# Attention of two heads at a time, and the state input of the S5 mixer on ScalarE's queue

## The chip, the cores and the metric

The kernel runs on one core of one Trainium2 chip. The time is the device time of one execution in microseconds (us). The engines are TensorE (PE; its weight loads are PEld), VectorE (DVE), ScalarE (ACT), GpSimd (POOL) and SyncE (SP), whose queue issues most of the DMAs.

## What is computed

Two blocks of a network over 512 tokens of 1024 features, in float32. The first pools, then runs a gated feed-forward layer with a short convolution. The second has two layers. Layer 0 mixes tokens by forgetting attention, layer 1 by an S5 state space model, and each ends in a gated feed-forward layer. What the change touches is the attention and the entry of S5:

```
def fox_mixer(h, w_in, b_f, q_gain, k_gain, w_out):      # 16 heads of 64
    proj = h @ w_in                                      # q, k, v, gate, f_logit
    q = rmsnorm(heads(q), q_gain); k = rmsnorm(heads(k), k_gain); v = heads(v)
    c = jnp.cumsum(log_sigmoid(f_logit + b_f), axis=1)
    for blk in range(seq_len // Q_BLOCK):                # 4 blocks of 128 queries
        s = einsum('bhqd,bhkd->bhqk', qb, kb) * scale + c[q] - c[k]
        s = where(mask, s, -inf)                         # causal
        p = softmax(s, axis=-1)
        outs.append(einsum('bhqk,bhkd->bhqd', p, vb))
    return (concatenate(outs) * sigmoid(gate)) @ w_out

def s5_mixer(h, w_in, ...):
    u = h @ w_in       # states from u, then outputs from the states and from u
    ...
    y = gelu(y + d_skip * u)
    return (y * sigmoid(y @ w_glu)) @ w_out
```

## The kernel before

Every large product is split in three passes: a weight tile is divided into a high and a low part (`w_hi` by ACT in `hi`, `w_lo` by DVE in `lo`), the activations into `hh` and `hl`, and PE runs high by high, high by low and low by high (`passes`, L1742 to L1744). A slot is one weight tile of 128x1024: 8 steps of 128 by three passes are 24 matmuls of 512 columns. Five slots lie in a ring (`RING`). SP loads slot n when slot n-5 is done, and `hi` and `lo` of slot n+3 are written beside slot n (`LEAD`).

Each engine runs its own program in the order in which it is written, with semaphores between them. In `fox` the loop over i takes the heads by pairs. A pair's q and k lie in `qk`, head 0 on partitions 0 to 63, head 1 on 64 to 127. For each i PE runs three slots of the next pair (n, n+1, n+2: q, k, gate), and between them the steps of the pair i, one head at a time:

- `scores(jj, head)`: for each of four query blocks `qb`, of 512, 128, 384 and 256 columns, three matmuls of q with k over 64 rows (L1989 to L1991), the causal mask over 128 rows (L1992), and the forget table `c_tab` over 48 rows (L1993). All five have one head's half of the rows, but the mask.
- DVE `row_max` (L1325), ACT `attend_exp` (L916), DVE `normalize` (L1335).
- `transposes` (L2005): ten blocks of 128x128 of `prob`, then ACT and DVE split them into `pt_hi` and `pt_lo`.
- `values`: 12 matmuls into bank 7, then DVE `head_out` multiplies with the gate and splits the result.
- `head_sums` (L2034): the sums of squares of q and k of the next pair, two float32 matmuls that give four records, after the scores of head 1. ACT then takes a logarithm and an exponential for the norm, DVE makes `qk` (`make_qk`).

`scores` of a pair waits for both halves of its `qk` (`qk_done`). After the last pair `fox_out` runs the output product.

POOL makes rotation tables for S5 beside this loop. SP stores one every second slot.

In `s5` the input product u comes out in 8 slots of 512 columns. `evict_u` (ACT) copies each to `us`. SP writes it to DRAM (`u_write`, L655) and reads it back in another order (`u_read`, L661) into `ub`. PE needs `ub` in `states(i)` (L2137) and `inside(i)` (L2147). DVE runs the recurrence between, and `across_two` (L2152) adds the states' outputs, with the two halves of the rows in turn. SP's queue also carries w1, turn, w3 (8 DMAs each, L645) and q2 tables, the weights, and the even trips of y (`y_write`, `y_read` with 8 DMAs; the odd ones are on ACT's queue). At the start of S5 SP first waits for all table stores and issues four w3 tables before the weight slots 1 to 4 of S5.

## Time and profile before

| | |
|---|---|
| runs shown | 1893.88, 1901.82, 1902.87 us (median 1901.82) |
| profiled execution | 1896.73 us, its span 1895.0 us |
| mean granted clock of TensorE in it | 0.937 |
| PE busy | 94% of the span |
| DVE, ACT, POOL busy | 55%, 34%, 12% |

Times in the profile count from the first instruction. The span is cut into stretches below, and for each the busy time of each engine and the granted clock of TensorE are read. The clock has two levels, 2.4 GHz (granted 1.00) and 1.2 GHz (0.50). A value between is a mean over the stretch. "xN" behind an engine's time counts its instructions, those that reach into the stretch included.

### The profile page before, as it was taken

What the parts mean: (1) busy time and instruction counts of PE and PEld (TensorE: products, weight loads), DVE (VectorE), ACT (ScalarE), POOL (GpSimd) and SP (SyncE); (2) the same over time, 40 slices, a digit from 0 to 9 for tenths busy, and PEclk for the clock granted to TensorE, in tenths of its full rate; (3) what the DMA queues carried; (4) which work ended last, traced back from release to release, by engine and by line L of the source; (5) the groups of instructions that cost most, each with busy time, mean ns of one, the idle gap of its engine ahead of it and who ended that gap; (6) DMA issues with size and microseconds to landing.
All of it is one profiled execution on the core that took longest, in us unless ns stands there. A gap on an engine that the chain in (4) does not pass through costs nothing.

```text
span 1895.0 us, 22168 instructions
## 1 busy us (share of the span) xinstructions
PE 1772.6 (94%) x8681; PEld 1466.2 (77%) x8681; DVE 1040.9 (55%) x1575; ACT 637.5 (34%) x1000; POOL 228.5 (12%) x757
## 2 busy tenths in 40 slices
PE   2749999999999999999999999997979999999998
PEld 2738888888787777777888888886868888888886
DVE  5988766676645555555734335665652653433323
ACT  3335433323434434343522222233213442222222
POOL 5001520000037423431000000000011000000000
PEclk7569999999999888888999999998969999999999
DMA  9443323334442111211322323445864233223332
GB/s 382 153 170 100 100 91 99 100 123 139 117 123 65 47 43 39 62 37 48 114 91 99 100 93 119 123 131 179 236 180 141 67 123 100 100 91 98 100 92 75
DMA packets 138151, 212.69 MB, mean 112 GB/s; under 512 B 29904, under 2 KB 104000, under 8 KB 134848
## 3 DMA queue, kind: packets, MB, share of 16 engines
q1 hardware_dynamic: 132864, 209.18, 34.9%
q10 hardware_dynamic: 5184, 2.10, 0.4%
q8 instruction: 69, 1.13, 0.2%
q14 instruction: 34, 0.28, 0.0%
HBM read 193.43 MB, written 17.82 MB: 111 GB/s over the span
## 4 chain that ended last, share of the span: by engine, by line
PE 81%; DVE 7%; DMA 4%; SPq 3%; ACT 2%; POOL 1%; issue 1%; ACTq 0%; DVEq 0%; PEldq 0%; POOLq 0%
PE bank L1742 24%; PE bank L1743 24%; PE bank L1744 24%; DMA u_scratch<-us 2%; SPq L645 2%; DVE ada L1161 1%; PE bank L1993 1%; DMA rcnt<-in_rcnt 1%; ACT prob L916 1%; DVE w_lo L1075 1%; PE bank L1989 1%; PE bank L1873 1%; PE bank L1782 1%; PE bank L2147 1%; DVE rinv L1325 1%
## 5 line engine op out<-in xcount | busy, mean ns | idle before, releaser
L1742 PE MATMUL bank<-hh,w_hi 128*128 128x512 f32 (+1 forms) x1440 | 560.9, 390 | 17.7 <-DVE w_lo L1075 14.0
L1743 PE MATMUL bank<-hl,w_hi 128*128 128x512 f32 (+1 forms) x1440 | 551.6, 383 | 0.0
L1744 PE MATMUL bank<-hh,w_lo 128*128 128x512 f32 (+1 forms) x1440 | 551.0, 383 | 0.0
L1075 DVE TENSOR_TENSOR w_lo<-raw,w_hi 128x1024 fp32r<-128x1024 f32 x264 | 318.4, 1223 | 241.7 <-ACT w_hi L732 238.3
L732 ACT ACTIVATE w_hi<-raw 128x1024 fp32r<-128x1024 f32 x264 | 278.7, 1057 | 394.9 <-PE bank L1744 123.9
L1742 PEld LDWEIGHTS bank<-hh,w_hi 128*128 128x128 f32 x1440 | 275.5, 191 | 74.3 <-DVE w_lo L1075 15.2
L1743 PEld LDWEIGHTS bank<-hl,w_hi 128*128 128x128 f32 x1440 | 275.0, 191 | 53.4 <-issue 3.0
L1744 PEld LDWEIGHTS bank<-hh,w_lo 128*128 128x128 f32 x1440 | 274.2, 190 | 52.8
L1742 PE MATMUL bank<-w_hi,hid 128*128 128x512 f32 x528 | 207.1, 392 | 0.0
L1744 PE MATMUL bank<-w_hi,hid 128*128 128x512 f32 x528 | 205.6, 389 | 0.0
L1743 PE MATMUL bank<-w_lo,hid 128*128 128x512 f32 x528 | 205.4, 389 | 0.0
L1221 DVE TENSOR_TENSOR scr<-scr,bank 128x512 f32<-128x512 f32 x44 | 30.3, 688 | 289.8 <-PE bank L1744 289.8
L1742 PEld LDWEIGHTS bank<-w_hi,hid 128*128 128x128 f32 x528 | 99.1, 188 | 22.1 <-issue 1.7
L824 ACT ACTIVATE scr<-bank 128x512 f32<-128x512 f32 x44 | 26.3, 598 | 266.8 <-PE bank L1744 266.8
L1744 PEld LDWEIGHTS bank<-w_hi,hid 128*128 128x128 f32 x528 | 99.1, 188 | 20.9
L1743 PEld LDWEIGHTS bank<-w_lo,hid 128*128 128x128 f32 x528 | 99.2, 188 | 20.2
L811 ACT ACTIVATE scr<-bank,convw 128x512 f32<-128x512 f32 x44 | 34.4, 781 | 139.3 <-PE bank L1744 139.3
L1737 POOL TENSOR_TENSOR hl<-yfm,hh 128x512 fp32r<-128x512 f32 x8 | 10.9, 1388 | 571.5 <-ACT hh L1004 571.5
L1197 DVE SCALAR_TENSOR_TENSOR scr<-bank,convw,scr 128x511 f32<-128x511 f32 x44 | 33.0, 749 | 64.6 <-ACT scr L811 64.6
L916 ACT ACTIVATE prob<-bank,nmax 128x128 f32<-128x128 f32 (+1 forms) x64 | 32.9, 526 | 105.2 <-DVE nmax L1327 105.2
L1161 DVE CUSTOM_DVE_ANT_0 ada<-ada,csil 128x1024 f32<-128x1024 f32 x48 | 57.6, 1255 | 12.6 <-DMA ada<-in_ada_w 12.4
L1594 POOL TENSOR_TENSOR turn_new<-turn_t 128x2 f32<-128x2 f32 (+2 forms) x192 | 55.4, 288 | 15.0
(271 smaller groups left out, 2204.0 us busy)
## 6 DMA issues: line engine op xcount, KB each, us to landing
raw<-in_up SPq DMA_DIRECT2D x132, 512.0 KB, 3.3
raw<-in_dn SPq DMA_DIRECT2D x60, 512.0 KB, 4.1
ada<-in_ada_w SPq DMA_DIRECT2D x24, 1024.0 KB, 9.6
raw<-in_fox_in SPq DMA_DIRECT2D x32, 512.0 KB, 3.9
raw<-in_s_w SPq DMA_DIRECT2D x24, 512.0 KB, 4.5
q_scratch<-q_tab SPq DMA_DIRECT2D x8, 512.0 KB, 4.3
w_scratch<-w_new SPq DMA_DIRECT2D x8, 512.0 KB, 5.1
raw<-in_fox_out SPq DMA_DIRECT2D x8, 512.0 KB, 3.7
```

Source lines behind the costliest of these rows:

```text
L645: sp.dma_start(w3[s::BLK, i % TABS, :, :], k_dram[i][:, :, at_s:at_s + P]).then_inc(w3_in[i % TABS], 16)
L732: act.activation(w_hi[:, n % RING, :], raw[:, n % RING, :], ACT.Copy).then_inc(hi_done, 1)
L811: act.activation(scr[:, 2 * s, :], bank[base + (2 * j + s) % 4][:, :], ACT.Identity, scale=convw[:, j, 4 * s + 1:4 * s + 2], bias=convw[:, ...
L916: act.activation(prob[:, P_AT[qb]:P_AT[qb] + w], S_AT[qb], ACT.Exp, bias=nmax[:, qb:qb + 1], accum_out=rsum[:, qb:qb + 1]).then_inc(exp_do ...
L1075: dve.tensor_tensor(w_lo[:, n % RING, :], raw[:, n % RING, :], w_hi[:, n % RING, :].bitcast(F32), ALU.subtract).then_inc(lo_done, 1)
L1161: dot = dve.tensor_tensor_reduce(wt, wt, csil[:, :], 1.0, 0.0, ALU.mult, ALU.add, accum_out=dots[:, 2 * b + t:2 * b + t + 1])
L1197: own.add(dve.scalar_tensor_tensor(c[:, 1:T], b[:, 0:T - 1], convw[:, j, 4 * s:4 * s + 1], c[:, 1:T], ALU.mult, ALU.add))
L1221: dve.tensor_tensor(p, scr[:, j % 2, :], bank[base + (2 * j + 1) % 4][:, :], ALU.mult)\
L1594: own.add(pool.tensor_tensor(out_, a, b, op))
L1742: pe.matmul(dst, w_h, r_h, start=first, stop=False, skip_group_check=True)
L1743: pe.matmul(dst, w_h, r_l, start=False, stop=False, skip_group_check=True)
L1744: return pe.matmul(dst, w_l, r_h, start=False, stop=last, skip_group_check=True)
```

## The change

The two heads of a pair now go through every step together.

- Scores: `two_scores` issues each matmul of head 0 and head 1 in turn, on rows 0 to 63 and 64 to 127, into different banks. The table comes before the mask. Block sizes are paired as (512, 512), (384, 256), (128, 384), (256, 128).
- Softmax in two groups: `WIDE` holds the two blocks of 512, `REST` the other six. Maxima, exponentials and reciprocals are made by group.
- All 20 transposes stand behind slot n+1, all 24 value matmuls behind slot n+2.
- The sum of squares of q stands in the middle of slot n+1, that of k behind the transposes. ACT and DVE make q before k is there.
- `head_out` handles both heads in one copy and one subtraction.
- In S5, ACT issues the write and the read of u. SP issues two w3 and two q2 tables before the weight slots 1 to 4, and waits for the table stores only behind a third w3 table.

```diff
-        S_AT = [bank[2][:, 0:P], bank[3][:, 0:2 * P], bank[2][:, P:4 * P], bank[4][:, :]]
+        def s_at(h, qb):
+            return (bank[4 + h][:, 0:P], bank[6][:, 2 * P * h:2 * P * h + 2 * P], bank[4 + h][:, P:4 * P],
+                    bank[2 + h][:, :])[qb]
...
+        WIDE, REST = [(0, 3), (1, 3)], [(0, 2), (1, 2), (0, 1), (1, 1), (0, 0), (1, 0)]
+        HS_BANK = [bank[7], bank[1]]
...
-            def u_write(i):
-                sp.wait_ge(ut_done, i + 1)
-                sp.dma_start(u_dram[i], us[:, i, :]).then_inc(u_out, 16)
-
-            def u_read(i):
...
             sp.wait_ge(slot_mm, S_S5I - TAIL)
             sp.wait_ge(turn_out, 16 * PAIRS // 2)
+            for i in range(2):
+                w1_load(i)
+                turn_load(i)
+            for i in range(2):
+                w3_load(i)
+                q2_load(i)
+            for idx in range(1, RING):
+                load_fm(S_S5I + idx, dram["s5_w"][idx])
+            w3_load(2)
             sp.wait_ge(k_out, 16 * KT)
             sp.wait_ge(w1_out, 16 * KT)
             sp.wait_ge(q_out, 16 * KT)
-            for i in range(2):
-                w1_load(i)
-                turn_load(i)
-            for i in range(3):
-                w3_load(i)
-                q2_load(i)
-            w3_load(3)
-            for idx in range(1, RING):
-                load_fm(S_S5I + idx, dram["s5_w"][idx])
             for i in range(KT):
                 load_fm(S_S5I + RING + i, dram["s5_w"][RING + i])
-                u_write(i)
                 if i >= 2:
                     w1_load(i)
-                u_read(i)
-                if i >= 2:
                     turn_load(i)
                 if i == 0:
+                    w3_load(3)
+                if i == 1:
+                    q2_load(2)
+                if i == 3:
                     q2_load(3)
                 if i == 5:
                     w3_load(4)
...
-                    if i >= 1:
-                        attend_pt(2 * i - 1)
                     if i >= 0:
-                        attend_exp(2 * i)
-                    hi(n + LEAD)
+                        attend_exp(i)
...
                         if nxt:
-                            act.wait_ge(hs_mm, 2 * nxt)
+                            act.wait_ge(qk_done, 2 * nxt)
                         act.activation(sq[:, 0, :], bank[0][:, :], ACT.Square).then_inc(sqh_done, 1)
-                    if i >= 0:
-                        attend_pt(2 * i)
+                    hi(n + LEAD)
+                    hi(n + 1 + LEAD)
                     if nxt is not None:
-                        hi(n + 1 + LEAD)
+                        head_scale(nxt, 0)
                         act.wait_ge(slot_mm, n + 2)
                         act.activation(sq[:, 1, :], bank[1][:, :], ACT.Square).then_inc(sqh_done, 1)
-                    else:
-                        hi(n + 1 + LEAD)
                     if i >= 0:
-                        attend_exp(2 * i + 1)
+                        attend_pt(i)
                     if nxt is not None:
+                        head_scale(nxt, 1)
                         hi(n + 2 + LEAD)
...
-                attend_pt(2 * KT - 1)
...
                 act.activation(us[:, i, :], bank[4 + i % 2][:, :], ACT.Copy).then_inc(ut_done, 1)
+                act.wait_ge(ut_done, i + 1)
+                act.dma_start(u_dram[i], us[:, i, :]).then_inc(u_out, 16)
+
+            def u_read(i):
+                act.wait_ge(u_out, 16 * (i + 1))
...
             def s5():
+                hi(S_S5I + LEAD)
                 for i in range(6):
-                    hi(S_S5I + i + LEAD)
                     evict_u(i)
+                    hi(S_S5I + i + 1 + LEAD)
+                    u_read(i)
                 gelu(0)
                 gelu(1)
                 y_write(act, 1)
-                hi(S_GLU + 1)
                 y_read(act, 1)
                 evict_u(6)
                 hi(S_GLU + 2)
+                u_read(6)
                 evict_u(7)
+                u_read(7)
                 high_y(0)
...
                     if i >= 1:
-                        pt_split(2 * i - 1)
+                        head_out(i - 1)
                     if i >= 0:
-                        row_max(2 * i)
-                    lo(n + LEAD)
-                    if i >= 0:
-                        normalize(2 * i)
-                    if i >= 1:
-                        head_out(i - 1, 1)
+                        row_max(i)
+                        normalize(i)
                     if nxt is not None:
                         copy_qk(nxt, 0, n)
-                    if i >= 0:
-                        pt_split(2 * i)
+                    lo(n + LEAD)
                     lo(n + 1 + LEAD)
                     if nxt is not None:
+                        make_qk(nxt, 0)
                         copy_qk(nxt, 1, n + 1)
-                    if i == KT - 1:
-                        row_max(2 * i + 1)
-                        head_out(i, 0)
-                        normalize(2 * i + 1)
-                    elif i >= 0:
-                        head_out(i, 0)
-                        row_max(2 * i + 1)
+                    if i >= 0:
+                        pt_split(i)
+                    if nxt is not None:
                         lo(n + 2 + LEAD)
-                        normalize(2 * i + 1)
-                    else:
-                        lo(n + 2 + LEAD)
-                    if nxt is not None:
-                        make_qk(nxt)
-                pt_split(2 * KT - 1)
-                head_out(KT - 1, 1)
+                        make_qk(nxt, 1)
+                head_out(KT - 1)
...
+            def score_ops(jj, h, qb):
+                r, cr = slice(HD * h, HD * h + HD), slice(HD * h, HD * h + 3 * HEADS)
+                w, dst, qs = P * (qb + 1), s_at(h, qb), slice(P * qb, P * qb + P)
+                yield pe.matmul(dst, qk[r, 0, qs], qk[r, 2, 0:w], start=True, stop=False)
+                yield pe.matmul(dst, qk[r, 0, qs], qk[r, 3, 0:w], start=False, stop=False)
+                yield pe.matmul(dst, qk[r, 1, qs], qk[r, 2, 0:w], start=False, stop=False)
+                yield pe.matmul(dst, sel[cr, 2 * jj + h, :], c_tab[cr, 0:w], start=False, stop=False)
+                yield pe.matmul(dst[:, w - P:w], ident_bf[:, :], causal[:, :], start=False, stop=True)
+
+            def two_scores(jj, qb0, qb1):
+                for first, second in zip(score_ops(jj, 0, qb0), score_ops(jj, 1, qb1)):
+                    pass
+                return second
+
+            def scores(jj):
                 pe.wait_ge(qk_done, 2 * jj + 2)
-                if hd:
-                    pe.wait_ge(exp_done, QB * hd)
-                for qb in (3, 0, 2, 1):
-                    if qb == 1 and hd:
-                        pe.wait_ge(pt_done, 3 * (hd - 1) + 1)
-                    w = P * (qb + 1)
-                    dst, qs = S_AT[qb], slice(P * qb, P * qb + P)
-                    pe.matmul(dst, qk[r, 0, qs], qk[r, 2, 0:w], start=True, stop=False)
-                    pe.matmul(dst, qk[r, 0, qs], qk[r, 3, 0:w], start=False, stop=False)
-                    pe.matmul(dst, qk[r, 1, qs], qk[r, 2, 0:w], start=False, stop=False)
-                    pe.matmul(dst[:, w - P:w], ident_bf[:, :], causal[:, :], start=False, stop=False)
-                    mm = pe.matmul(dst, sel[cr, hd, :], c_tab[cr, 0:w], start=False, stop=True)
...
+                if jj:
+                    pe.wait_ge(pt_done, 5 * jj)
+                two_scores(jj, 3, 3).then_inc(s_mm, 1)
+                two_scores(jj, 2, 1).then_inc(s_bank, 1)
+                two_scores(jj, 0, 2)
+                pe.wait_ge(s_bank, jj + 1)
+                two_scores(jj, 1, 0).then_inc(s_mm, 1)
+
+            def transposes(jj):
+                pe.wait_ge(p_done, 2 * QB * (jj + 1))
...
+                        at_ = P_AT[qb] + P * kb
+                        mm = pe.transpose(t_at(h, kb)[:, P * (qb - kb):P * (qb - kb) + P], prob[:, h, at_:at_ + P],
+                                          ident[:, :])
+                    return mm
+                block_row(0, 0).then_inc(pt_mm, 1)
+                block_row(1, 0).then_inc(pt_mm, 1)
+                for h in range(2):
+                    block_row(h, 1)
+                    block_row(h, 3).then_inc(pt_mm, 1)
+                block_row(0, 2)
+                block_row(1, 2).then_inc(pt_mm, 1)
...
+                pe.wait_ge(sqh_done, 2 * nxt + t + 1)
+                pe.matmul(HS_BANK[t][:, :], blk64[:, :], sq[:, t, :], start=True, stop=True).then_inc(hs_mm, 1)
...
                     if i >= 0:
-                        scores(i, 0)
-                    if i >= 1:
-                        values(i - 1, 1)
+                        scores(i)
                     if nxt is None:
-                        pe.wait_ge(qf_done, 2 * KT)
-                        pe.wait_ge(g_done, KT)
-                        for idx in range(2):
-                            pe.wait_ge(lo_done, S_FO + idx + 1)
-                            pe.wait_ge(o_done, 4 * idx + 4)
-                            out_part(idx, (0, 1))
-                        transposes(i, 0)
-                        scores(i, 1)
-                        values(i, 0)
-                        pe.wait_ge(lo_done, S_FO + 3)
-                        pe.wait_ge(o_done, 12)
-                        out_part(2, (0, 1))
-                        transposes(i, 1)
-                        continue
+                        break
...
+                        pe.wait_ge(z_ready, 1)
                     fm_slot(n, bank[0][:, :], hh, hl)
+                    pe.wait_ge(lo_done, n + 2)
+                    if nxt:
+                        pe.wait_ge(ln_done, 2 * nxt)
+                    if i >= 1:
+                        pe.wait_ge(o_done, i)
+                    fm_part(n + 1, bank[1][:, :], hh, hl, 0, 4)
+                    head_sum(nxt, 0)
+                    fm_part(n + 1, bank[1][:, :], hh, hl, 4, KT).then_inc(slot_mm, 1)
                     if i >= 0:
-                        transposes(i, 0)
-                    if nxt:
-                        pe.wait_ge(qf_done, 2 * nxt)
-                        pe.wait_ge(sqh_done, 2 * nxt)
-                    fm_slot(n + 1, bank[1][:, :], hh, hl)
-                    if i >= 0:
-                        values(i, 0)
-                        scores(i, 1)
-                    head_sums(nxt)
-                    pe.wait_ge(qf_done, 2 * nxt + 1)
+                        transposes(i)
+                    pe.wait_ge(qf_done, 2 * nxt + 2)
+                    head_sum(nxt, 1)
                     fm_slot(n + 2, bank[0][:, :], hh, hl)
                     if i >= 0:
-                        transposes(i, 1)
+                        pe.wait_ge(ln_done, 2 * nxt + 2)
+                        values(i)
...
                 for idx in range(3):
-                    out_part(idx, (2,))
-                values(KT - 1, 1)
+                    pe.wait_ge(lo_done, S_FO + idx + 1)
+                    out_part(idx, (0, 1))
+                transposes(KT - 1)
+                values(KT - 1)
                 for idx in range(3):
-                    out_part(idx, (3,)).then_inc(slot_mm, 1)
+                    out_part(idx, (2, 3)).then_inc(slot_mm, 1)
```

On PE, the first scores of the pair 0 before (head 0 alone, the banks named):

```order
L1989 MATMUL bank4<-qk_133 128x512
L1990 MATMUL bank4<-qk_133 128x512
L1991 MATMUL bank4<-qk_133 128x512
L1992 MATMUL bank4<-causal_75,ident_bf_74 128x128
L1993 MATMUL bank4<-c_tab_141,sel_147 128x512
L1989 MATMUL bank2<-qk_133 128x128
```

and the same place now:

```order
L1986 MATMUL bank2<-qk_137 128x512
L1986 MATMUL bank3<-qk_137 128x512
L1987 MATMUL bank2<-qk_137 128x512
L1987 MATMUL bank3<-qk_137 128x512
L1988 MATMUL bank2<-qk_137 128x512
L1988 MATMUL bank3<-qk_137 128x512
L1989 MATMUL bank2<-c_tab_145,sel_146 128x512
L1989 MATMUL bank3<-c_tab_145,sel_146 128x512
L1990 MATMUL bank2<-causal_75,ident_bf_74 128x128
L1990 MATMUL bank3<-causal_75,ident_bf_74 128x128
L1986 MATMUL bank4<-qk_137 128x384
L1986 MATMUL bank6<-qk_137 128x256
```

Each row of head 0 is now followed by the row of head 1 into another bank.

On SP, from the last turn table to the weights of S5 (`w_164` is w3, `q_165` is q2), before:

```order
L637 DMA turn<-turn_scratch 128x512
L645 DMA w_164<-k_scratch 16x8x128 x8
L650 DMA q_165<-q_scratch 128x1024
L645 DMA w_164<-k_scratch 16x8x128 x8
L650 DMA q_165<-q_scratch 128x1024
L645 DMA w_164<-k_scratch 16x8x128 x8
L650 DMA q_165<-q_scratch 128x1024
L645 DMA w_164<-k_scratch 16x8x128 x8
L491 DMA raw<-in_s_w 128x1024 [waits slot_mm] x5
```

and now:

```order
L655 DMA turn<-turn_scratch 128x512
L663 DMA w_163<-k_scratch 16x8x128 x8
L668 DMA q_164<-q_scratch 128x1024
L663 DMA w_163<-k_scratch 16x8x128 x8
L668 DMA q_164<-q_scratch 128x1024
L509 DMA raw<-in_s_w 128x1024 [waits slot_mm] x4
L663 DMA w_163<-k_scratch 16x8x128 x8
L509 DMA raw<-in_s_w 128x1024 [waits q_out,slot_mm,w1_out,k_out]
```

Sixteen w3 issues and one q2 issue moved behind the four weight slots.

On ACT, around the copies of u(6) and u(7), before:

```order
L480 DMA yfm<-y_scratch 16x8x64 x8
L995 ACTIVATE us<-bank 128x512
L732 ACTIVATE w_hi<-raw 128x1024
L995 ACTIVATE us<-bank 128x512
L1004 ACTIVATE hh<-yfm 128x512 x2
```

and now:

```order
L498 DMA yfm<-y_scratch 16x8x64 x8
L999 ACTIVATE us<-bank 128x512
L1001 DMA u_scratch<-us 128x512
L740 ACTIVATE w_hi<-raw 128x1024
L1007 DMA ub<-u_scratch 128x8x64
L999 ACTIVATE us<-bank 128x512
L1001 DMA u_scratch<-us 128x512
L1007 DMA ub<-u_scratch 128x8x64
L1017 ACTIVATE hh<-yfm 128x512 x2
```

The write and the read of u stand on ACT's queue, ahead of the high parts of y.

## Rows read from the trace of the kernel before

**Rows 1.** The page: granted clock of TensorE in 40 equal slices, in tenths.
```profile
PEclk7569999999999888888999999998969999999999
```

**Rows 2.** Busy time by stretch: seven attention pairs, their end, S5.
```profile
core 0: us, PE busy (x) PEld busy (x) DVE busy (x) ACT busy (x) POOL busy (x), PEclk, DMA share, GB/s
586.61:856.26 269.65, 258.84 (x1109) 197.53 (x1109) 151.72 (x296) 116.36 (x240) 110.68 (x456) 0.87 0.16 49
856.26:901.40 45.14, 44.59 (x193) 35.81 (x194) 21.37 (x42) 13.12 (x30) 7.97 (x40) 0.85 0.13 39
1300.00:1440.00 140.00, 116.09 (x949) 102.46 (x948) 70.19 (x153) 30.32 (x45) 6.29 (x5) 0.82 0.64 187
```

**Rows 3.** The same view, TensorE alone: steps of a pair at clock 1.00, last at 0.54.
```profile
715.98:716.99 1.01, 1.01 (x11) 1.00 0.00 0
716.99:722.54 5.55, 5.55 (x27) 1.00 0.31 94
722.54:724.49 1.95, 1.95 (x13) 1.00 0.32 76
724.49:728.61 4.12, 4.12 (x22) 1.00 0.37 123
728.61:736.08 7.47, 7.46 (x29) 1.00 0.00 0
740.25:746.79 6.54, 6.54 (x20) 0.54 0.01 1
```

**Rows 4.** Timeline of TensorE: where two blocks of scores begin (start, duration, line, operands).
```profile
724.49 0.49 PE L1989 MATMUL bank<-qk 64*128 64x512 f32 x1
...
725.88 0.22 PE L1989 MATMUL bank<-qk 64*128 64x128 f32 x1
```

**Rows 5.** Timeline of TensorE in S5: 64-row records in turn, 128-row records.
```profile
1359.20 4.07 PE L2152 MATMUL bank<-xs,q 64*128 64x63 f32 x64
...
1370.35 3.79 PE L2147 MATMUL bank<-ub,w 128*128 128x64 f32 x32
```

**Rows 6.** What TensorE waited for: over the span, and (last row) in the seven pairs.
```profile
PE bank L1742 <- DVE w_lo L1075: 15.5, 3, 12.2
PE bank L2137 <- DMA ub<-u_scratch: 10.2, 2, 5.8
...
PE bank L1989 <- DVE qk L1356: 9.3, 7, 2.5
```

**Rows 7.** Groups of DVE and ACT in the seven pairs: count, busy us, mean ns.
```profile
L1325 DVE TENSOR_REDUCE rinv<-bank 128x1 f32<-128x512 f32 (+3 forms) x56 | 23.6, 484 | 40.9 <-PE bank L1993 40.9
L1340 DVE TENSOR_TENSOR pt_lo<-bank,pt_hi 128x512 fp32r<-128x512 f32 (+1 forms) x40 | 22.5, 594 | 5.0 <-ACT pt_hi L924 4.3
L1335 DVE TENSOR_SCALAR prob<-prob,rinv 128x128 f32<-128x128 f32 (+3 forms) x56 | 18.3, 390 | 0.5
...
L916 ACT ACTIVATE prob<-bank,nmax 128x128 f32<-128x128 f32 (+3 forms) x56 | 28.8, 526 | 93.2 <-DVE nmax L1327 93.2
L916 ACT ACTIVATION_READ_ACCUMULATOR prob<-bank,nmax 128x1 f32 x56 | 11.4, 203 | 0.0
```

**Rows 8.** SP's queue at the start of S5 and at u(6): start, duration, what is issued.
```profile
1285.39 5.07 SPq L645 DMA_DIRECT2D w<-k_scratch  x8
...
1307.58 18.59 SPq L491 DMA_DIRECT2D raw<-in_s_w  x5
...
1383.49 0.43 SPq L655 DMA_DIRECT2D u_scratch<-us  x1
```

**Rows 9.** Timeline of ACT in S5.
```profile
1311.81 1.06 ACT L732 ACTIVATE w_hi<-raw 128x1024 fp32r<-128x1024 f32 x1 [12.40 <-DMA raw<-in_s_w]
...
1372.89 0.60 ACT L995 ACTIVATE us<-bank 128x512 f32<-128x512 f32 x1 [6.90 <-issue]
```

**Rows 10.** Timeline of POOL in S5.
```profile
1385.16 2.98 POOL L1737 TENSOR_TENSOR hl<-yfm,hh 128x512 fp32r<-128x512 f32 x2 [519.06 <-ACT hh L1004]
```

More of the change, by code:

```diff
@@ L1329, in normalize @@
[L1329 to L1341 removed]
+                dve.tensor_tensor(vo_lo[:, jj, :], z, vo_hi[:, jj, :].bitcast(F32), ALU.subtract).then_inc(o_done, 1)
```

219 lines of the change are left out of this document (105 added, 114 removed).

## The prediction

> **What bounds the kernel now.** I read the clock row of the page first, then the busy time by stretch, then TensorE alone inside one stretch. TensorE is the bound: busy 94% of the span. The clock row [rows 1] is at 9 or above nearly everywhere, with dips at the start, in the attention (slices 14 to 19) and in S5 (slices 28 to 30). The change touches the last two places. The reader should compare three numbers in each row of [rows 2]: length, PE busy, clock. In the seven pairs from 586.61 to 856.26 us PE is busy 258.84 of 269.65 us, so 10.8 us are idle, and the clock is 0.87, so some 0.13 x 269.65 = 35 us go to the lower level. A pair takes 269.65 / 7 = 38.5 us.
>
> The steps of a pair at clock 1.00 are in [rows 3]: ten transposes 1.01, a slot 5.55, values of one head 1.95, scores of one head 4.12, and two sums of squares with the slot behind them 7.47, so the sums alone 7.47 - 5.55 = 1.92. A pair needs 3 x 5.55 + 2 x 1.01 + 2 x 1.95 + 2 x 4.12 + 1.92 = 32.7 us. The other 5.8 us are idle time (1.5) and the slow clock.
>
> Where does the clock fall? In 14 of the 16 score steps the granted clock went to 0.50 inside the step or right behind it; the last row of [rows 3] is such a step, 6.54 us for what takes 4.12. What ran before each fall was matmuls with only 64 or 48 of the 128 rows, each block with a change of row shape. There were 12 falls in the seven pairs, so one costs 35 / 12 = 2.9 us.
>
> **The scores.** One head's scores have 1280 columns in four blocks. A slot gives 5.55 / 24 = 0.23 us per 512 columns. Four passes over 1280 columns are 2.30 us and four masks, at 0.11 us each (an estimate from [rows 5], where a record with a load of 128 columns takes 3.79 / 32 = 0.118), 0.44. Of the 4.12 us 1.38 remain, 0.35 per block, for the changes of shape; the first block shows it: 724.49 to 725.88 is 1.39 us for 0.92 + 0.11 [rows 4]. Now two heads share a pass. If the halves run side by side, a pass takes as long as the wider one: 512 + 384 + 384 + 256 = 1536 columns, by four 2.76 us, eight masks 0.88, four blocks at 0.35 1.38: 5.0 us for the pair instead of 8.24. If they don't, it is 2 x 2.74 + 1.38 = 6.9, at worst 8.24. Do they? The trace has the pattern in S5 [rows 5]: 64 records in turn on the two halves took 4.07 us, 64 ns each, while 32 records on all rows, with the same weight width and one column more, took 3.79 us, 118 ns each. Two ran in the time of one. I take 5.0 and keep 4.2 (half the shape changes gone, since table and q share a half) and 6.9 as ends.
>
> **The pair.** 16.65 + 2.02 + 3.90 + 1.92 + 5.02 = 29.5 us at clock 1.00. It holds only if nobody is late:
> - Transposes need all probabilities. From the start of the scores DVE has `head_out` of the pair before (four operations at 0.59, with settling 2.9), eight maxima at 0.48 (3.9), ACT eight exponentials at 0.53 + 0.20 (5.8), DVE eight products at 0.39 (3.1) [rows 7], and 1 us of small ones: 16.7 us if nothing overlapped, about 13.6 with the two groups overlapping. PE asks at 5.0 + 11.1 + 0.96 = 17.1. Both fit, the first by 0.4 us.
> - `values` ask at 17.1 + 2.0 + 1.0 + 5.6 = 25.7. The transposes end at 19.1 and five subtractions at 0.59 behind them are done by some 22.
> - The next `qk` is ready near 26: the k sum ends at 20.1, two ACT operations 1.4, then behind `lo` three of DVE. PE asks at 29.5. Now this wait takes 9.3 us in seven pairs [rows 6]; it goes, since the gate slot and the values stand ahead.
> - POOL's tables and SP's stores keep their rhythm of one per two slots. POOL is busy 110.68 us in seven pairs, 15.8 per pair of 29.5.
>
> Seven pairs are 206.6 us instead of 269.7: **-63**. This takes the idle time and the slow clock as gone. The full array is used in the scores, and in the trace the step of S5 that takes the halves in turn ran at clock 1.00 [rows 5], though its records are as sparse. The sums inside a slot have matmuls around them.
>
> **Before and behind the loop.** For the first pair PE now waits for a square and a copy before the k sum, where it waited for the square: +0.7. Behind the loop, 856.26 to 901.40 us is 45.1 now [rows 2]. It becomes scores 5.0, four slots' worth of output product 22.2, transposes 2.0, values 3.9, and a new wait: two `lo` (1.2 each) stand on DVE between the products and the five subtractions, so `pt_lo` ends about 18.5 us after the start where PE is through at 15.3: 3.2. With one fall of the clock (2) 38.4: **-6.7**.
>
> **S5, the start.** PE waited 12.2 us for the low part of the first new weight slot [rows 6]. SP issued four w3 tables of 5.07 us each before it, and the weight at 1307.58 [rows 8]; ACT had it at 1311.81 [rows 9], PE could start at 1314.8. Two w3 and a q2 table fewer, and no wait for the last stores (2.7 us), put the issue at 1294. Then the ring is the limit: the slot comes free near 1296, its weight lands about 4.2 us later, high and low part take 2.3, PE starts at 1303. About 11.5 us, plus some of the slow clock: **-12**. The bounds are 8 (the moved w3 tables share the DMA engines with the weights) and 14.
>
> **S5, the end.** PE waited 5.8 and 4.4 us for u(6) and u(7) [rows 6]. ACT had copied u(6) at 1372.89 [rows 9], SP wrote it at 1383.49 [rows 8], behind 16 w3 issues and a y trip. ACT now writes it at once: read back by 1382, before PE asks (1384.8). u(7) lands near 1389. But the next waits come up. The high parts of y(0) and y(1) stand behind `u_read(7)`, and POOL needs 2.98 us for two [rows 10], so PE waits some 3 us there. Then SP's chain y(2), q2, w3(6), w3(7) still ends near 1411, so `inside(7)` ends at about 1414 instead of 1427.7. The clock falls in these waits as before. I take **-12**, bounds 3 and 18. New on ACT is that it stands in `u_read(i)` until the write has landed, some 6 us; behind it are only the next copy and the next `w_hi`, both with a slot to spare.
>
> The Trainium skill bears on this step ("DMA: Bandwidth & Descriptors", "Issuing engines are not separate DMA queues"): DMAs of all issuing engines run on the same 16 DMA engines, so another engine saves only issue time. By it the trip itself gets no shorter; here the row on SP shows that what is saved is 10 us of queueing.
>
> **Sum.** -63 - 6.7 + 0.7 - 12 - 12 = -93 us. The span 1895.0 becomes 1802, the execution (1.7 us more) 1804. The median shown is 5.1 us above the profiled one. I take half of that: **1806 us**.
>
> **Rivals.**
> - The clock still falls once per pair at the scores. For it: eight masks and eight changes of shape remain, and the step is longer than one head's. Against it: [rows 5]. Price 8 x 2.9 = 23: 1829 us. 19%.
> - The clock falls at the 20 transposes in a row. Ten held 1.00 [rows 3]; with the k sum behind them the new stretch is 3 us. Price again 8 x 2.9: 1829. 5%. The Trainium skill says so ("TensorE: Matmul & The Clock Gate", "Part 4: PE-mode transpose"): the full clock doesn't engage for transposes. The trace speaks against it for ten, and shows no twenty.
> - The halves don't overlap in this format with 512 columns: scores 6.9 us, +15, and the clock falls, +23: 1844. 5%.
> - In S5 only the start is won, since the y trips take u's place as what is waited for: +12, 1818. 11%.
> - Slower than before: the softmax chain. All transposes of a pair wait for both heads, where half a pair could go before. If the chain were over 17.1 us, PE would wait in every pair. From 17.1 + 93 / 8 = 28.7 us on the gain is gone and the time above 1902; DVE and ACT would have to take 70% more than the serial sum. 4%, and 2% for an end near 1902.
> - My forecast: 54%.
>
> **Range.** Downward, scores at 4.2 give 6, S5 up to 8, the wait behind the loop 4: 1788. Upward it takes in the clock rivals and S5: 1832. Left out are the missing overlap and the slow chain, and tails. A difference under 0.5% can't be told from none. Faster 0.94, same 0.02, slower 0.04.
>
> **What would show it.** Right: 29 to 30 us from one pair's scores to the next; scores of 4.5 to 5.2 us, the second record of each couple starting within some 10 ns of the first; clock above 0.97 in the pairs; no wait for `qk` and none for `prob`; PE's wait for `w_lo` at the start of S5 under 2 us; no wait for `ub`, but one for POOL's `hl` and one for w3. Wrong: couples 0.23 us apart (no overlap), clock 0.50 behind each score step, or PE idle before the transposes with DVE busy.

## The result and the profile after

| | before | changed kernel |
|---|---|---|
| median of 4 runs | 1898.57 us (1893.88 to 1902.87) | **1800.72 us** (1799.64 to 1805.31) |
| span of the profiled run | 1895.0 us | 1798.6 us |
| mean granted clock | 0.937 | 0.969 |

The ratio of the times is 0.949, 95% interval 0.946 to 0.952: 5.1% faster, 1800.7 us where 1806 was forecast. Five later runs of the same kernel gave a median of 1800.8 us (1799.77 to 1801.3).

The clock row of the page of the changed kernel, to be laid beside [rows 1]: the dips in the attention are gone, those of S5 are smaller.

```profile
PEclk7579999999999999999999999999989999999999
```

Busy time by stretch in the changed kernel (length, then busy time and count for PE, PEld, DVE, ACT, POOL, then clock, DMA share, GB/s). The first row is the seven pairs from the first pair's scores to the last pair's and answers to the first of [rows 2]; the second is what lies behind the loop, up to the end of the output product; the third is S5 from the end of the work ahead of its first weight slot to its first output matmul.

```profile
590.70:791.26 200.56, 200.56 (x1120) 160.96 (x1120) 142.43 (x276) 117.78 (x233) 115.10 (x443) 1.00 0.21 66
791.26:849.97 58.71, 56.27 (x293) 46.28 (x292) 38.51 (x70) 27.41 (x60) 9.29 (x40) 1.00 0.19 57
1227.62:1379.13 151.51, 136.20 (x1082) 116.86 (x1081) 88.78 (x175) 46.17 (x60) 10.28 (x8) 0.95 0.65 194
```

The same view of the kernel before for S5, between the same two instructions:

```profile
1302.61:1475.52 172.91, 147.37 (x1081) 128.10 (x1081) 88.75 (x175) 47.87 (x63) 10.95 (x8) 0.85 0.59 174
```

The seven pairs went from 269.65 to 200.56 us, 28.65 us per pair instead of 38.5; TensorE shows no idle time in them and the clock is 1.00. The stretch behind the loop was 68.69 us (856.26 to 924.95) and is 58.71. S5 was 172.91 and is 151.51; note that TensorE's *busy* time there fell from 147.4 to 136.2 us for the same 1081 matmuls.

What TensorE waited for in the changed kernel (us in total, times, longest), first from 560 to 900 us, then in S5; it answers to [rows 6]:

```profile
PE bank L1748 <- DVE pt_lo L1361: 2.4, 1, 2.4
PE bank L2044 <- DVE qf L1365: 1.4, 1, 1.4
```
```profile
PE bank L2150 <- DMA w<-k_scratch: 6.3, 2, 3.4
PE bank L2140 <- DMA w<-w_scratch: 2.9, 1, 2.9
PE bank L1748 <- POOL hl L1743: 1.6, 1, 1.6
PE bank L2140 <- DMA ub<-u_scratch: 1.5, 1, 1.5
PE bank L1748 <- DVE w_lo L1091: 1.1, 1, 1.1
```

Where the 96.4 us between the two spans lie:

| stretch | forecast | measured |
|---|---|---|
| up to the first pair's scores (586.61, 590.70) | +0.7 | +4.1 |
| seven pairs | -63 | -69.1 |
| behind the loop | -6.7 | -10.0 |
| S5, from the eight transposes ahead of its first slot to where `states(6)` is asked for (83.2, 72.7 us) | -12 | -10.6 |
| S5, from there to the end of `across_two(6)` (52.8, 41.7 us) | -12 | -11.1 |

The rest, +0.3, is spread over the gate slots; from 849.97 us to S5, and behind S5, the two traces are alike to 0.1 us.

### The profile page after: what moved, and what is told of

It is laid out like the page before. It is cut to its first block, busy times and chain, and to the rows that moved or that the text cites. A ratio compares the mean times of both kernels' runs of the same rounds, so it can differ in the third digit from the quotient of the medians.

```text
span 1798.6 us, 22087 instructions
## 1 busy us (share of the span) xinstructions
PE 1692.3 (94%) x8681; PEld 1410.4 (78%) x8681; DVE 1031.1 (57%) x1551; ACT 639.8 (36%) x992; POOL 237.0 (13%) x757
## 4 chain that ended last, share of the span: by engine, by line
PE 86%; DVE 6%; DMA 3%; POOL 1%; ACT 1%; SPq 1%; issue 1%; ACTq 0%; DVEq 0%; PEldq 0%; POOLq 0%
PE bank L1748 26%; PE bank L1750 26%; PE bank L1749 26%; DVE ada L1177 2%; DMA rcnt<-in_rcnt 1%; PE bank L1788 1%; PE bank L2013 1%; PE bank L1879 1%; PE bank L2044 1%; PE bank L2150 1%; PE bank L1986 1%; DMA u_scratch<-us 1%; DVE w_lo L1091 1%; SPq L663 1%; DMA raw<-in_fox_in 1%
## 5 line engine op out<-in xcount | busy, mean ns | idle before, releaser
L1600 POOL TENSOR_TENSOR turn_t<-turn_new 128x2 f32<-128x2 f32 (+2 forms) x192 | 57.4, 299 | 0.0
```

The costliest lines, as they stand in the source:

```text
L1600: own.add(pool.tensor_tensor(out_, a, b, op))
```

## Experiments

Times are medians; a ratio is to the kernel before run on the same chip in between. The kernel before had medians of 1898.57, 1895.74, 1896.17 and 1896.64 us in the four sets of runs (the result's, then three below), so two times from different sets can differ by some 3 us without a cause in the kernels. A stretch is read from the one profiled run of each version.

### The two parts apart

`att_only` has the attention of the changed kernel and S5 of before; `s5_only` the reverse.

> The attention as in the changed kernel, S5 as before. Theory (the two parts are independent, and the sum of the traces holds): 1898.6 + 4.1 - 69.1 - 10.0 = 1823.6 us, 1821 to 1827, with pairs of 28.65 us and a granted clock of 1.00 from the first pair on up to S5, where the 12.2 us of waiting for the first weight slot and the 5.8 and 4.4 us for ub come back. Rival (part of what the S5 rows show is a gift of the attention: with transfers and the clock in another phase S5 got shorter by itself): below 1818. Rival (S5's edits hid a loss that the attention makes): above 1830.

> S5 as in the changed kernel, the attention as before. Theory (independent parts): 1898.6 - 21.4 = 1877.2 us, 1874 to 1880, with one short wait for the low part of the first weight slot (about 1 us), 1.5 us for ub(1), 2.9 us for w1 and 6.3 us for w3. Rival (parts interact): outside of that, and then att_only is off by as much the other way.

Measured: `att_only` 1818.28 us, ratio 0.960 (0.957 to 0.962); `s5_only` 1874.98 us, 0.990 (0.987 to 0.994). The gains add: 4.0% and 1.0% against 5.1% together. `s5_only` came where it was expected, and its S5 takes 151.2 us. In `att_only` the attention is the same to the hundredth of a us; its busy time by stretch, the seven pairs and S5:

```profile
590.21:790.77 200.56, 200.56 (x1120) 160.95 (x1121) 142.12 (x276) 117.77 (x233) 115.06 (x442) 1.00 0.21 66
1227.15:1396.65 169.50, 141.97 (x1081) 123.15 (x1082) 85.64 (x175) 47.71 (x63) 10.03 (x8) 0.88 0.60 178
```

`att_only` is 5 us faster than expected. 3.4 of them are in its second row: S5 with the code of before takes 169.5 us here and took 172.9 before. It waits longer (26.0 us against 24.0) but spends 41 us at the lower clock instead of 51. So 3.4 of the 21.4 us that S5 lost came with the attention, as the first rival has it (below 1818, and the median is 1818.28). S5 depends on how its waits meet the clock; that comes back below.

### The order of the two heads' matmuls

```
 def two_scores(jj, qb0, qb1):
-    for first, second in zip(score_ops(jj, 0, qb0), score_ops(jj, 1, qb1)):
-        pass
-    return second
+    for h, qb in ((0, qb0), (1, qb1)):
+        for mm in score_ops(jj, h, qb):
+            pass
+    return mm
```

> The changed kernel, but in each couple of score blocks the five matmuls of head 0 are issued first and then the five of head 1: the same matmuls, no longer in turn on the row halves. Theory (the overlap comes from the order, and the clock fell because matmuls on half the rows ran one after the other): the score step goes from 4.36 to 8.2 us or more and the clock falls once per pair again: 8 x 3.9 + 8 x 2.9 = +54, about 1855 us. Rival 1 (the clock was lost to the idle time in the pairs, 10.8 us before, not to the half rows): the step takes 8.2 us at clock 1.00, +31, 1832 us. Rival 2 (neighbouring blocks overlap by themselves wherever they stand): 1801 us, step unchanged.

Measured: 1855.57 us, ratio 0.979 (0.976 to 0.983), against 1855 expected of the first theory. TensorE's timeline at one couple of 512-column blocks in the changed kernel (start, duration, line, operands, count). Each row is two matmuls, one per head; the rows stand 0.23 us apart, what one 512-column matmul takes:

```profile
648.35 0.39 PE L1987 MATMUL bank<-qk 64*128 64x512 f32 x2
648.58 0.39 PE L1988 MATMUL bank<-qk 64*128 64x512 f32 x2
648.81 0.40 PE L1989 MATMUL bank<-c_tab,sel 48*128 48x512 f32 x2
649.14 0.29 PE L1990 MATMUL bank<-causal,ident_bf 128*128 128x128 bf16 x2
649.36 0.44 PE L1986 MATMUL bank<-qk 64*128 64x384 f32 x2
```

The same place in `heads_apart`: the same matmuls, one per 0.23 us, and the slot behind them at the lower clock (0.43 us apart, 671.01 to 671.44):

```profile
662.04 0.39 PE L1988 MATMUL bank<-qk 64*128 64x512 f32 x1
662.28 0.40 PE L1989 MATMUL bank<-c_tab,sel 48*128 48x512 f32 x1
662.61 0.23 PE L1990 MATMUL bank<-causal,ident_bf 128*128 128x128 bf16 x1
662.76 0.49 PE L1986 MATMUL bank<-qk 64*128 64x512 f32 x1
...
671.01 0.63 PE L1749 MATMUL bank<-hl,w_hi 128*128 128x512 f32 x1
671.44 0.63 PE L1750 MATMUL bank<-hh,w_lo 128*128 128x512 f32 x1
```

Its seven pairs:

```profile
590.09:839.25 249.16, 249.16 (x1120) 196.80 (x1121) 142.43 (x276) 117.76 (x233) 110.77 (x442) 0.88 0.17 53
```

The overlap comes from the order alone. And the clock fell in or behind each score step again, 58.0 us at half rate in the seven pairs, though TensorE had no idle time in them at all. So the falls need no idle time; what the 10.8 us of it added in the kernel before, no run takes apart. Nor is it the length of the step alone: before, one head's step took 4.12 us at full clock and 14 of 16 had a fall; in turn the step takes 4.36 us and none of eight has one. 249.2 is 200.6 + 29.0 (half of 58.0) + 19.6, the last being 2.8 us per pair for the missing overlap: a step of about 7.2 us at full clock. The clock is worth more than the overlap. That the total met the expectation is partly luck: the step lost 2.8 us per pair and not 3.9, the clock cost 29.0 us in seven pairs and not 20 (7 x 2.9), and S5 took 3.6 us more than in the changed kernel (155.1 us).

### What the score step's 4.36 us are made of

```
-    yield pe.matmul(dst, sel[cr, 2 * jj + h, :], c_tab[cr, 0:w], start=False, stop=False)
-    yield pe.matmul(dst[:, w - P:w], ident_bf[:, :], causal[:, :], start=False, stop=True)
+    yield pe.matmul(dst, sel[cr, 2 * jj + h, :], c_tab[cr, 0:w], start=False, stop=True)
```

> The changed kernel without the eight causal masks of a pair's scores (the softmax then takes in later tokens, which is what is left out). They are the only matmuls of the step that use all rows. Theory (the mis-sized term of the score step is the change of shape between row halves and all rows, and it comes with the masks): the step goes from 4.36 to about 2.8 us, the bare 12 x 0.23, -12 for eight pairs, about 1789 us. Rival (masks cost only their own 0.11 us each, and the rest of the changes of shape lies between blocks): 3.5 us, -7, about 1794 us. The clock stays at 1.00 in the pairs by both.

Measured: 1792.83 us (1791.02 and 1794.64); the score step takes 2.75 us. That is the bare 12 x 0.23: without the masks nothing remains for changes of shape between the blocks. From the timeline of TensorE in `no_mask`, the last pass of one couple and the first of the next, with no gap between them:

```profile
699.24 0.39 PE L1988 MATMUL bank<-qk 64*128 64x512 f32 x2
699.47 0.40 PE L1989 MATMUL bank<-c_tab,sel 48*128 48x512 f32 x2
699.71 0.34 PE L1986 MATMUL bank<-qk 64*128 64x384 f32 x2
```

Eight masks cost 4.36 - 2.75 = 1.61 us, 0.20 each with the changes they bring. The first theory holds for the step, and the seven pairs are 11.0 us shorter (189.5 us). The time fell by 8 us, not 12: S5 of this run took 155.9 us, 4.4 more than in the changed kernel, with 15.7 us of waits and 20.5 us of slow clock.

### Forty transposes in a row

```
 def transposes(jj):
     pe.wait_ge(p_done, 2 * QB * (jj + 1))
+    for kb in range(QB):
+        for h in range(2):
+            block_row(h, kb)
```

> The changed kernel with the 20 transposes of a pair done twice in a row, into the same banks (the second set is the one that is used). Theory (the clock doesn't mind transposes): each pair 2.0 to 2.2 us longer, all of it at a granted clock of 1.00, 8 x 2.1 = +17, about 1817 us. Rival (the rule that transposes don't hold the full clock, with 20 in a row just too few to show it): with 40 in a row, 4.3 us, the clock falls in or behind them once per pair, 8 x 2.9 more, about 1841 us.

Measured: 1817.14 us (1816.86 and 1817.42). The forty and the whole of the seven pairs, by stretch:

```profile
699.26:703.63 4.37, 4.37 (x42) 4.37 (x40) 2.34 (x5) 2.09 (x5) 0.07 (x2) 1.00 0.53 150
590.37:806.45 216.08, 216.08 (x1262) 176.22 (x1262) 142.91 (x276) 118.69 (x233) 114.79 (x444) 1.00 0.20 62
```

109 ns per transpose and a clock of 1.00 throughout. Transposes don't pull the clock down here, at four times the count that [rows 3] showed. The Trainium skill ("TensorE: Matmul & The Clock Gate", "Part 4: PE-mode transpose") says that the full clock doesn't engage for them; for forty transposes in a row among dense matmuls this run disagrees.

### The sum of squares behind its slot

```
-    fm_part(n + 1, bank[1][:, :], hh, hl, 0, 4)
-    head_sum(nxt, 0)
-    fm_part(n + 1, bank[1][:, :], hh, hl, 4, KT).then_inc(slot_mm, 1)
+    fm_slot(n + 1, bank[1][:, :], hh, hl)
+    head_sum(nxt, 0)
```

> The changed kernel with the sum of squares of q behind its slot instead of in the middle of it, so that sum, 20 transposes and the other sum stand in a row. Theory (the middle of a slot isn't needed: the sum costs 0.8 us in either place, and qk is asked for far later): within 2 us of 1800.7, pairs of 28.5 to 28.8 us at clock 1.00. Rival 1 (the clock needs dense matmuls between the sums): 3.1 us of sparse work in a row, a fall per pair, +23, about 1824 us. Rival 2 (the place in mid-slot is what gets qk ready in time): a wait for qk of 1 to 2.5 us per pair, +8 to +20.

Measured: 1821.89 us, ratio 0.961 (0.958 to 0.963): 21 us slower than the changed kernel. The middle of the slot matters, nearly as the second rival had it in size, but by another tile than `qk`. The sums and transposes in a row, with 1.9 us of waiting among them, brought no fall in six of the seven pairs; in one the clock was low for 3.4 us shortly behind that wait (at 801.4). Its stretch of seven pairs and what TensorE waited for in it:

```profile
594.58:811.90 217.32, 203.87 (x1121) 162.19 (x1120) 141.31 (x276) 117.09 (x233) 106.56 (x431) 0.99 0.20 61
```
```profile
PE bank L2044 <- DVE qf L1365: 13.4, 7, 1.9
```

It isn't `qk` that is late but the second sum: it may only start when DVE has copied k off its bank. Of the 22.6 us between the spans of the two profiled runs 16.8 lie in the seven pairs (13.4 of them this wait), 3.9 ahead of the first pair and 2.2 in S5. DVE's timeline shows why the copy is late:

```profile
704.90 0.75 DVE L1370 SCALAR_TENSOR_TENSOR qf<-qf,qk_gain,hr 128x512 f32<-128x512 f32 x1 [3.09 <-ACT hr L939]
705.69 0.43 DVE L1373 CAST qk<-qf 128x512 fp32r<-128x512 f32 x1
706.15 0.69 DVE L1375 TENSOR_TENSOR qk<-qf,qk 128x512 fp32r<-128x512 f32 x1
706.76 0.68 DVE L1365 COPY qf<-bank 128x512 f32<-128x512 f32 x1
```

The copy stands behind `make_qk(nxt, 0)`, and that waits 3.1 us for the root of the *first* sum, against 0.6 in the changed kernel. A sum 2.7 us earlier, in mid-slot, gets this chain done under the second half of the slot and the transposes. My theory that the place didn't matter fell.

### S5: SP's new order without ACT's queue

`u_on_sp` keeps SP's new order of tables and weights and gives the trips of `u` back to SP, in the place of its loop that they had before. ACT's part of S5 is that of before, the places of `hi` included.

```
 for i in range(KT):
     load_fm(S_S5I + RING + i, dram["s5_w"][RING + i])
+    u_write(i)
     if i >= 2:
         w1_load(i)
+    u_read(i)
+    if i >= 2:
         turn_load(i)
 ...                    # and ACT's part of S5 as before
```

> The changed kernel with SP's new order of tables and weights, but the trips of u written and read back by SP again, in the same place of its loop as before. Theory (two separate gains in S5: the order gives the start, ACT's queue gives u(6) and u(7) at the end): the start stays at 1 us of waiting, u(6) is written only behind y_read(0), so some 7 us later, and the waits for ub come back: +4 to +11, about 1808 us. Rival 1 (the order alone does it, since w1(6) and w3(6) are waited for at the same places anyway): within 2 us of 1800.7. Rival 2 (SP now stands in each write's landing in front of the weight slots, so the start is lost too): above 1815.

Measured: 1813.98 us, ratio 0.958 (0.955 to 0.961); S5 takes 166.7 us. What TensorE waited for in S5:

```profile
PE bank L2142 <- DMA ub<-u_scratch: 15.4, 4, 7.6
PE bank L1750 <- POOL hl L1745: 1.6, 1, 1.6
PE bank L1750 <- DVE w_lo L1093: 1.5, 1, 1.5
```

The first weight slot stayed won (1.5 us for the first low part, 12.2 in [rows 6]), and u(6) and u(7) are waited for again, 7.6 and 3.9 us. The other two of the four waits for ub, 3.1 and 0.8 us, lie at the start of S5 (1260.2 and 1267.9), where the changed kernel waits 1.5 us: ACT's queue saves 2.4 us there as well. The mechanism of the first theory held for the end and its size didn't: 13 us, not 4 to 11. With the waits the time at the lower clock rose from 13.7 to 41.0 us.

### Versions against the waits that are left

`both_orders` moves three things in the changed kernel, `y_first` two more, `relay` gives one table to POOL:

```
 # both_orders: SP
 w3_load(4)
 y_write(sp, 0)
+w1_load(6)             # was behind y_read(sp, 0)
 w3_load(5)
 y_read(sp, 0)
...
 y_write(sp, 2)
 q2_load(5)
+w3_load(6)             # was behind y_read(sp, 2)
 y_read(sp, 2)
 w3_load(7)
 # both_orders: DVE, behind the last pair
+pt_split(i)            # was behind the two lo
 lo(n + LEAD)
 lo(n + 1 + LEAD)
 # y_first, in addition
 w1_load(6)
+y_read(sp, 0)          # SP: before w3_load(5)
 w3_load(5)
 evict_u(7)
 high_y(0)
 high_y(1)
+u_read(7)              # ACT: was before high_y(0)
 # relay, in addition: w3_load(6) off SP; on POOL behind its second hl
+pool.wait_ge(w3_mm, 3)
+for s in range(BLK): pool.dma_start(w3[s::BLK, 2, :, :], ...)
```

> The changed kernel with three moves against the waits that its trace shows: SP loads w1(6) between w3(4) and w3(5) instead of behind both and y_read(0); w3(6) is issued before y_read(2), where SP stood 6 us waiting for y(2); and behind the last pair DVE does the five subtractions of the probabilities ahead of two lo. Theory (each wait was SP's or DVE's order alone): 2.4 us behind the loop, 2.9 for w1(6), 3.4 and 1 to 3 for w3 and up to 6 us of slow clock in their wake: 1785 to 1791 us. Rival (behind each stands the next: POOL's hl for y(0) and y(1) ends at 1301.2 in the trace, 2 us behind where PE would ask): 2.4 + 1.5 + 4, about 1793 us, with a wait for hl in place of w1.

> The changed kernel itself, as the neighbour of the two versions that follow, since the version with three moves differed from it by less than its own scatter. By any theory 1800.7 us, 1797 to 1805, with a profile whose waits in S5 differ by a few us from run to run if they hang on how transfers meet, and by less than 1 us if they hang on the order of issue alone.

> The version with three moves, and two more against the waits that it still shows (1.9 us for POOL's hl, 3.8 us for w3(7)): SP reads y(0) back before it issues w3(5), and ACT makes the high parts of y(0) and y(1) before it waits for the landing of u(7). Theory (hl was late by the order alone): no wait for hl before the first gate slots, -1.9, but ub(7) or w3(7) takes part of it: 1790 to 1796 us. Rival (the waits come from transfers that meet on the DMA engines, so order moves them only from tile to tile): 1796 to 1800 us, with the same 9 to 10 us of waiting in S5 in other places.

> As y_first, and w3(6) is issued by the idle POOL behind its second hl, so that SP issues only w3(7) ahead of y_read(2). Theory (SP's 5 to 6 us of issuing per w3 table is what the last wait hangs on): the 3.8 us for w3(7) and the fall of the clock behind it (6.8 us at half rate) go, -6, about 1787 us. Rival (POOL needs longer for its eight issues than SP, or its third hl is held up by them): a wait for w3(6) or for hl of 2 to 8 us in its place, 1793 to 1803 us.

Measured: the changed kernel again 1800.80 us (1799.77 to 1801.3); `both_orders` 1798.37 (1794.87 to 1810.38), `y_first` 1800.86 (1798.02 to 1803.95), `relay` 1806.38 (1802.32 to 1808.31). None is told apart from the changed kernel in the right direction; `relay` is slower by 5.6. The trace of `both_orders` is of its run of 1795.51 us, 2.9 below its median. Why so little came of it is seen in S5 of each. Length, sum of TensorE's waits over 0.45 us, and time at the lower clock, all from the trace:

| kernel | S5, us | waits | at the lower clock | length less waits and clock |
|---|---|---|---|---|
| before | 172.9 | 24.0 | 51.2 | 130.6 |
| `att_only` | 169.5 | 26.0 | 41.0 | 131.0 |
| `u_on_sp` | 166.7 | 18.5 | 41.0 | 131.0 |
| `relay` | 158.1 | 11.7 | 34.1 | 131.9 |
| `s5_only` | 151.2 | 9.1 | 23.9 | 131.9 |
| changed kernel | 151.5 | 14.0 | 13.7 | 132.2 |
| changed kernel, again | 151.4 | 10.8 | 20.5 | 132.3 |
| `y_first` | 149.6 | 8.3 | 20.5 | 131.9 |
| `both_orders` | 147.5 | 12.1 | 6.8 | 132.5 |

The last column is the length less the waits and less half the slow time in which TensorE worked. It stays at 130.6 to 132.5, so the two terms explain nearly all of what sets these lengths apart. The two rows of the changed kernel show how far one trace can be trusted: 3.2 us of waits and 6.8 us of slow clock apart, at the same length. So `y_first` is best laid beside the changed kernel run again, which is of its own set: 2.5 us less of waits, the same slow time, S5 shorter by 1.8 us. In its list of waits one of 4.2 us is left where `states(7)` begins:

```profile
PE bank L2143 <- issue: 4.2, 1, 4.2
PE bank L1751 <- POOL hl L1746: 1.6, 1, 1.6
PE bank L2143 <- DMA ub<-u_scratch: 1.5, 1, 1.5
```

In `relay` that wait is 7.2 us. "issue" names no releaser, but `states(7)` waits for only three things, and the trace has the times of each. In `y_first` TensorE starts at 1308.22. u(7) had landed at 1301.03, and DVE had been through with what it asks for by 1297.03; what came last is w1(7), issued by SP at 1300.64 and 7.5 us on its way, the longest of its eight loads:

```profile
1308.22 1.08 PE L2143 MATMUL bank<-ub,w 128*64 128x64 f32 x15 [4.23 <-issue]
```
```profile
1300.64 0.71 SPq L649 DMA_DIRECT2D w<-w_scratch  x1
```
```profile
DMA to landing us min/median/max: 4.4/5.7/7.5
```

In `relay` SP issued it earlier, at 1299.26, and it took 11.3 us, up to 1310.55; TensorE starts at 1310.64. The eight transfers of w3(6) that POOL issued from 1298.23 on landed in the same time, from 1304.76 to 1309.67. That they slowed w1(7) fits, but no run takes it apart. Whether the waits would sink further if less were in flight is open, too.

## Why the prediction was right, point by point

**The bound and the seven pairs.** Right. -69.1 against -63. The price of the clock, read as 35 us from the mean clock of [rows 2], was right: the trace of before has 68.3 us at the lower clock in the seven pairs, half of which is 34.1. The 10.8 us of idle time went as well. `heads_apart` shows that one head's half-row matmuls behind the other's bring the clock down without any idle time.

**The score step.** The mechanism was right, the size 5.0 was too long: 4.36, nearer to the lower end 4.2. The term at fault is the change of shape. I had read 0.35 us per block off [rows 4] and kept it for four couples, 1.38 us beside masks of 0.11. `no_mask` shows that there is no such cost between couples. What there is comes with each mask, 0.20 us in all. 2.75 + 1.61 = 4.36. The 0.64 us make 4.5 in seven pairs, most of the 6 us by which the forecast fell short. Both signs that I had named, a step of 4.5 to 5.2 us and pairs of 29 to 30, were missed by this (4.36 and 28.65); the others of the pairs came: the second record of the first couple starts 4 ns behind the first, the clock is 1.00, and nothing is waited for. The Trainium skill ("TensorE: Matmul & The Clock Gate", "Why this matters for your kernels") has matmuls of few rows run at the same time when they lie in different row groups; the rows above agree, at 512 columns.

**Nobody late in the pairs.** Right, with more to spare than I had thought. TensorE asked for the probabilities 16.3 us after the scores' start (648.01, 664.29), not 17.1. In the last pair it already asks after 12.7 us (791.26, 803.92) and still doesn't wait; the last product ends at 803.26. So the softmax takes 12.0 us where I had 13.6 with the groups overlapping and 16.7 in series: the deadline has 4 us to spare. `sum_behind` shows that another margin is thin: 2.7 us of delay of one sum cost 1.9 us per pair. I hadn't listed that chain, sum to root to `make_qk` to the next copy, at all.

**Before the loop.** Wrong, +4.1 for +0.7. 1.05 us are there before the attention begins; from the forget logits (562.83, 563.88) to the scores it is 3.0. The wait that I priced at 0.7 measured 1.4, and another 0.9 us in front of the first slot wasn't in the sum. In the pairs the transposes stand between slot and k sum; ahead of the first pair there are none.

**Behind the loop.** -10.0 for -6.7. The term that failed is "with one fall of the clock (2)": the clock stayed at 1.00. But that is how this run fell out. In the second profile of the same kernel, and in those of `u_on_sp` and `no_mask`, the clock is low for 3.4 us here; the stretch in `after_again`:

```profile
795.00:850.00 55.00, 52.54 (x252) 0.97 0.18 53
```

The scores give another 0.6. The wait was 2.4 for 3.2, near enough, and its reason was wrong. I put it down to the two `lo` on DVE. In `both_orders`, with the five subtractions ahead of them, it is still 2.1:

```profile
803.42 2.35 PE L2016 MATMUL bank<-ident,prob 128*128 128x128 f32 x20
807.89 0.50 PE L1751 MATMUL bank<-pt_hi,vo_hi 128*128 128x512 f32 x1 [2.11 <-DVE pt_lo L1363]
```

It is the chain transposes, ACT's five copies, DVE's five subtractions itself, with no TensorE work placed over it.

**S5, the start.** -10.6 for -12. Right: 1.1 us of waiting where 12.2 were. The new 1.5 us for ub(1) is what the sum lacked, against the sign of no wait for ub; ACT stands in the landing of u(0) (1239.33 to 1243.59) before it copies u(1) at 1244.06, the serial trip that I had called harmless. `u_on_sp` shows that the order on SP alone wins the wait for the low part.

**S5, the end.** -11.1 for -12: the size was right by luck, for its working was wrong. I said that waits would shrink and "the clock falls in these waits as before". The view by stretch, from where `states(6)` is asked for to the end of `across_two(6)`, before and then after:

```profile
1384.79:1437.57 52.78, 41.85 (x292) 37.74 (x293) 18.81 (x38) 6.30 (x11) 5.90 (x4) 0.61 0.62 187
```
```profile
1299.25:1340.94 41.69, 31.62 (x293) 27.76 (x293) 19.47 (x39) 5.41 (x9) 4.63 (x4) 0.84 0.69 212
```

The idle time is the difference of length and busy time: 10.9 and 10.1 us, all but the same. 10.2 of the 11.1 us are busy time, and the clock went from 0.61 to 0.84. The wait for u went, as forecast; but the next in line took its place, 2.9 us for w1(6) and 6.3 for w3(6) and w3(7). SP's queue shows the first: w1(6) is issued at 1296.85, behind two tables and the trip of y.

```profile
1285.87 5.10 SPq L663 DMA_DIRECT2D w<-k_scratch  x8
1291.02 5.30 SPq L498 DMA_DIRECT2D yfm<-y_scratch  x8
1296.36 0.44 SPq L509 DMA_DIRECT2D raw<-in_s_w  x1
1296.85 0.43 SPq L649 DMA_DIRECT2D w<-w_scratch  x1
```

I had named w3; of w1(6) I had said nothing, and POOL's `hl`, which I expected there, was hidden behind it: in `both_orders`, with w1(6) in time, 1.9 us for `hl` stand in its place. (The 1.6 us for `hl` in the list lie at the next slots and stood there before, too.) What was really won is that the same amount of waiting no longer holds the clock down for 41 us around it, but for 13.7. Why waits in other places do this, no run takes apart.

The writes of u(0) and u(1) from ACT take 4.3 and 6.2 us to land, where those from SP took 4.0 and 5.9; what is saved is the time in SP's queue. The trace agrees with what the prediction cited from the Trainium skill ("DMA: Bandwidth & Descriptors", "Issuing engines are not separate DMA queues"). `relay` let a third engine issue, with POOL done in 4.4 us, and won nothing.

**The rivals.** The clock at the scores and at twenty transposes: both out, by a clock of 1.00 and by `transposes_twice`. No overlap: what it would have been is `heads_apart`, 1855.6 us; I had priced it at 1844. The missing part is the clock, 29 us in seven pairs where I had 23 in eight, and 7.2 us for the step where I had 6.9. "Only the start is won": not so, by the 11.1 us at the end. `u_on_sp` shows about what it would have been, 1814 where I had 1818. The softmax chain: not reached.

## What to carry to other kernels

A matmul with half the rows can cost more than its columns: one after the other, such matmuls here also took the clock from the dense work behind them, and in turn on both halves they cost half and the clock stayed. Read a stretch's idle time and its clock apart before you say what a wait is worth: at the end of S5 ten microseconds of waiting went with 41 us at the lower clock in one kernel and with 13.7 in the other. And when a small operation is moved, follow what waits for its *result* on each engine up to the next operation that was queued behind: here a sum of less than 1 us moved by half a slot cost 21 us.

## What the runs showed of the hardware beyond what I expected

- Two matmuls of 64 rows and 512 columns on different row halves take 0.23 us together, what one takes. A full-row mask of 128 columns between them costs 0.20 us, of which its 128 columns are about 0.06 (0.23 / 4, an estimate).
- Without such masks, couples with different column counts follow each other with no gap: 12 x 0.23 = 2.76 us, measured 2.75.
- Forty transposes in a row, 4.36 us, held clock 1.00. Sums, twenty transposes and a wait of 1.9 us in a row brought one short fall in seven pairs (clock 0.99 over them).
- In its first profile the changed kernel ran from 142 to 1303 us, 1160 us, without one fall of the clock; in the second it fell once on the way, for 3.4 us at 809.7. S5, with 8 to 14 us of waits, had 7 to 34 us at the lower level in versions that differ in the order of transfers and small copies and, in `relay`, in who issues eight of them.
- The same load, w1(7), landed after 7.5 us in `y_first` and after 11.3 in `relay`; the medians of the eight w1 loads are 5.7 and 6.1.
